# Products that nothing reads, put into TensorE's waits of a three-layer mixer network

## The chip, the cores and the metric

One core of one Trainium2 chip runs the whole network in one launch. The metric is the device time of an execution in microseconds; before the change it is 1105.38 us (median of 3 runs, 1104.76 to 1110.9).

## What is computed

One sequence of 256 tokens, width 1024, in f32, through three layers. Layer 0 ("first block") mixes with a gated linear recurrence, a gated linear attention and an eight-head block attention; layers 1 and 2 ("second block") mix with a delta-rule recurrence (RWKV-7), four heads of dilated attention and four heads of latent attention. Each layer ends in a gated feed-forward part of width 2816. Layer 0 norms what each half adds, layers 1 and 2 norm only what each half reads.

```python
def first_block(x, ...):                       # layer 0
    h = rms_norm(x, pre_mix_norm)
    x = x + rms_norm(hybrid_mixer(h, ...) @ w_out, post_mix_norm)
    h = rms_norm(x, pre_ffn_norm)
    f = (silu(h @ w_ffn_gate) * (h @ w_ffn_up)) @ w_ffn_down
    return x + rms_norm(f, post_ffn_norm)

def second_block(x, positions, ...):           # layers 1 and 2
    for l in range(2):
        h = rms_norm_2(x, attn_norm_g[l])
        pa, pb, pc = split_sizes(h @ w_in[l], (A_PROJ, B_PROJ, C_PROJ))
        y = [rwkv7_mixer(pa, ...), dilated_mixer(pb, ...), mla_mixer(pc, ...)]
        x = x + concatenate(y) @ w_out[l]
        h = rms_norm_2(x, ffn_norm_g[l])
        x = x + (silu(h @ ffn_w_gate[l]) * (h @ ffn_w_up[l])) @ ffn_w_down[l]
    return rms_norm_2(x, final_norm_g)
```

## The kernel before

Activations are held transposed, width on the 128 partitions in 8 tiles (`KT`), tokens (`T` = 256) in the free dimension. Each dense product with weights is made of three fp32r products (`product`, L433 to L442): high half of the weights by high half of the activations, high by low, low by high. The weights come from memory as 148 chunks of up to 1 MB (`STREAM`) through a ring of three buffers: SP issues the load, ACT writes the high half (`w_hi`, L1040), DVE the low half (`w_lo`, L1455; L2045 for the two halves of the first chunk), PE multiplies, and then the buffer is free again. The rest (inverse, heads, norm sums, rotations) is done in plain f32 products, each of which is two MATMUL records in the trace.

The order on each engine is written out by hand, one instruction list per engine, tied by step counters: `V` counts steps of DVE, `A` of ACT, `M` of PE. `pe.wait_ge(V.sem, V.at(...))` holds PE, and all behind it in PE's list, until DVE has marked that step.

- The start: `as_they_come` runs the first chunk's products as pairs of activation tiles and the halves of the chunk come in (L441).
- `norm_sum` (L462 to L471) sums squares over partitions with a product by ones; for "mixed" and "fed" in layer 0 it is followed by ACT's inverse root (L1052, L1054), DVE's norm, residual and low half (L1499, L1437, L1505), and then by the first products of the next part.
- `rwkv(l)` holds the recurrence. Eight 64x64 matrices per chunk of tokens are inverted by doubling, levels n = 1 to 5 in two groups q: first products (L817), then other work that `beside_inverse(l, n)` puts there, then the products L825 and L830, then DVE subtracts (L1437) and the next level may begin. At n = 2 the work beside is the latents' products `up(0)`, `up(1)` (L441), for which PE waits for `c_lo`; before them DVE splits a chunk and makes the latents' low half, after them it does rotations. Level 6 is L839 and L846.
- The heads: `attention(l, i)`, i = 0 to 9, is a pipeline over eight heads (`attend`): scores of head i (L989, L990 for the four narrow heads, L993 to L996 for the wide ones), three transposes of head i-1 (L564 to L566), values of head i-2 (L572, L573). Between scores and transposes DVE takes the maximum (L1560 to L1565), ACT the exponential (L1115, L1117), DVE scales (L1547 to L1551), and ACT copies the transposed rows (L1040). attention 0 to 3 stand beside levels 5 and 6 of the inverse, 4 to 6 around the first chunk of the state (c = 0; L876, L888/L889, L899/L901/L912/L913), 7 to 9 around the second.

Of the kernel before, what the change touches and what calls it, by code (L numbers as in the profile page):

```python
# [36 lines left out]
P = 128  # L37
D = 1024
KT = D // P
T = 256  # L40
# [184 lines left out]
def program(nc, ins, out, plan):  # L225


    with ExitStack() as ctx:
        def sb(name, shape, dt=F32):
            return ctx.enter_context(nc.sbuf_tensor(name, shape, dt))  # L230
# [90 lines left out]
        AT2 |= area(0, dict(att_l=(2, 384), att_p=(2, 384)))[0]  # L321
        cq_hi, cq_lo = h_hi[:, 0:3, :], h_lo[:, 0:3, :]
        small = sb("small", [P, 96])
        ANG, _ = area(8192 + T, dict(p=(T,), ang=(2, T), n=(T,)))
        pos = arena[:, 8192:8192 + T].bitcast(I32)

# [108 lines left out]
        def _(pe):  # L435
# [15 lines left out]
            H = [lambda k: h_hi[:, k, :], lambda k: h_lo[:, k, :]]  # L451
            MX = [lambda k: mix_hi[:, k, :], lambda k: mix_lo[:, k, :]]
            IDENT, ONES, BONES = C("ident"), C("ones"), C("bones")

            def norm_sum(l, what, into=6):

# [284 lines left out]
            def rwkv(l):  # L741
# [66 lines left out]
                    last.then_inc(M.sem, M.mark(l, "inv0", q))  # L808
                project(l, 8)
                for n in range(1, 6):  # L810
                    for q in range(2):

                        pe.wait_ge(V.sem, V.at(l, "inv_bt", n, q))
                        pe.wait_ge(A.sem, A.at(l, "inv0", q)) if n == 1 else pe.wait_ge(V.sem, V.at(l, "inv_x", n - 1, q))
                        for m in range(4 * q, 4 * q + 4):
                            for h in HALVES:
                                last = pe.matmul(quads(q)[h, m % 4, 0:64], BT[h, m, :], Xm[h, m, :],  # L817
                                                 start=True, stop=True)
                        last.then_inc(M.sem, M.mark(l, "inv_y", n, q))
                    beside_inverse(l, n)  # L820
                    for q in range(2):
                        pe.wait_ge(A.sem, A.at(l, "inv_y", n, q))
                        for m in range(4 * q, 4 * q + 4):
                            for h in HALVES:
                                last = pe.matmul(blocks(quads(2 + q)[h, m % 4, 0:64], n, 1), Y[h, m, :],  # L825
                                                 blocks(XT[h, m, :], n, 1), start=True, stop=True)
                        last.then_inc(M.sem, M.mark(l, "inv_zt", n, q))
                        for m in range(4 * q, 4 * q + 4):
                            for h in HALVES:
                                last = pe.matmul(blocks(quads(q)[h, m % 4, 0:64], n, 0), XT[h, m, :],  # L830
                                                 blocks(Y[h, m, :], n, 0), start=True, stop=True)
                        last.then_inc(M.sem, M.mark(l, "inv_z", n, q))
                    if n >= 5:
                        attention(l, 2 * n - 9)
# [32 lines left out]
                for c in range(TT):  # L867
# [11 lines left out]
                    if c:  # L879
                        mean_of(0)  # L880
                    attention(l, 4 + 3 * c)
                    pe.wait_ge(A.sem, A.at(l, "r", c))
                    if c == 0:
                        pe.wait_ge(V.sem, V.at(l, "inv_xt", 6, 1))
# [41 lines left out]
            def beside_inverse(l, n):  # L926

                b = AT2
                CQ = [lambda k: cq_hi[:, k, :], lambda k: cq_lo[:, k, :]]
                CKV = [lambda k: cq_hi[:, 2, :], lambda k: cq_lo[:, 2, :]]  # L930

                def up(i):


                    c = CHUNK[l, "uq" if i < 3 else "ukv", 0]
                    if i in (0, 3):
                        split(pe, c)
                    if i >= 2:
                        pe.wait_ge(A.sem, A.at(l, "up", i - 2))
                    if i < 3:  # L940
                        for t in range(2):
                            last = product(pairs(4 + i % 2)[:, t, :], tile_of(c, 2, 768, (2 * i + t) * P), range(2), CQ)
                    elif i < 5:
                        for t in range(2):
                            last = product(pairs(4 + i % 2)[:, t, :], tile_of(c, 1, 1024, (2 * (i - 3) + t) * P), [0],
                                           CKV)
                    else:
                        s, t = c % RING, i - 5
                        last = product(bank[4 + i % 2][:, :],
                                       [lambda k, p=p: p[:, 2, t * P:(t + 1) * P] for p in (cq_hi, cq_lo)], [0],  # L950
                                       [lambda k, p=p: p[:, s, 512:1024] for p in (w_hi, w_lo)])
                    last.then_inc(M.sem, M.mark(l, "up", i))

                if n == 1:

                    pe.wait_ge(V.sem, V.at(l, "in", 7))
                    pe.wait_ge(A.sem, A.at(l, "rkv"))
                    pe.wait_ge(A.sem, A.at(l, "kb_turned"))
                    pe.matmul(bank[6][:, :], C("rot_b"), B2["bq"].rearrange("p a b -> p (a b)"), start=True, stop=True)
                    pe.matmul(bank[7][:, :], C("rot_b"), B2["bk"].rearrange("p a b -> p (a b)"), start=True, stop=True)\  # L960
                        .then_inc(M.sem, M.mark(l, "b_rot"))
                if n == 2:
                    pe.wait_ge(V.sem, V.at(l, "c_lo"))
                    up(0)
                    up(1)
                if n == 3:

                    pe.wait_ge(V.sem, V.at(l, "rotated", 0))
                    pe.matmul(bank[6][:, 0:T], C("dup")[0:64, :], B2["krope"][0:64, :], start=True, stop=True)
                    pe.matmul(bank[6][:, T:2 * T], C("dup_rot")[0:64, :], B2["krope"][0:64, :], start=True, stop=True)\  # L970
                        .then_inc(M.sem, M.mark(l, "k_rot"))
                    for i in range(2, 5):
                        up(i)
                if n == 4:
                    pe.wait_ge(V.sem, V.at(l, "rotated", 1))
                    pe.matmul(bank[7][:, :], C("rot_c"), b["qr"].rearrange("p a b -> p (a b)"), start=True, stop=True)\
                        .then_inc(M.sem, M.mark(l, "q_rot"))
                    up(5)
                    up(6)
                if n >= 5:  # L980
                    attention(l, 2 * n - 10)

            def attention(l, i):
# [27 lines left out]
                    pe.wait_ge(V.sem, V.at(l, "b_lo"))  # L1011
                attend(l, i, 8, scores, value, out_bank)

            for l in range(LAYERS):
                if l:
                    pe.wait_ge(mats, 16 * l)
# [9 lines left out]
                        w_out(l, m, (0, 1) if m < 2 else range(KT))  # L1026
                if l == 0:
                    norm_sum(l, "mixed")
                ffn(l)
                if l == 0:  # L1030
                    norm_sum(l, "fed")
            norm_sum(LAYERS, "final")


# [396 lines left out]
        def _(dve):  # L1431
# [605 lines left out]
                    after_v("angles" if (i, s, n) == (1, 1, 7) else f"angle_{i}_{s}_{n}")  # L2037


            dve.wait_ge(x_loaded, 32)  # L2040
            def first_lo(h):

# [173 lines left out]
```

## Time and profile before

| what | value |
|---|---|
| median of 3 runs | 1105.38 us (1104.76 to 1110.9) |
| profiled execution, its own time | 1106.32 us |
| its span, first to last instruction | 1104.4 us |
| mean granted TensorE clock | 0.954 |
| PE, DVE, ACT busy | 95%, 62%, 46% |
| HBM read | 154 MB, 140 GB/s over the span |

The profile is of one execution. Its page has the busy times and, in 40 slices of 27.6 us, the granted clock (9 stands for 90% and more). A matmul's record is longer than the distance to the next one, since products are pipelined; the distance between starts is the pace. Lines are those of the kernel before.

### The profile page before, as it was taken

The numbers are of one execution on the slowest core, as the hardware profiler recorded it, in microseconds if no ns is written. First come the engines' busy times: TensorE is split into PE (matmuls) and PEld (weight loads), VectorE is DVE, ScalarE is ACT, GpSimd is POOL, SyncE is SP. The second block draws the span as 40 slices with busy tenths as digits, with TensorE's granted clock in tenths as the row PEclk, the third lists the DMA queues.
The fourth block names the chain that finished last, engine by engine and source line by source line (L and its number), as shares of the span: only waits on it lengthen the run. The fifth ranks groups of instructions, "written<-read, shape, count | busy, mean of one in ns | idle before, by whom it ended". The sixth has DMA issues, their size and how long they took to land. (4 is left out here: it accounts for less than half of the span.)

```text
span 1104.4 us, 20079 instructions
## 1 busy us (share of the span) xinstructions
PE 1052.7 (95%) x8728; PEld 989.1 (90%) x8728; DVE 684.1 (62%) x1079; ACT 503.8 (46%) x663; POOL 4.1 (0%) x9
## 2 busy tenths in 40 slices
PE   5999989999997998999999999999899999999996
PEld 5898889999997997769999999998776799999996
DVE  5867476775567877444665555579653456655554
ACT  5475464444436543233644443466233455444332
POOL 0000000000000000000000000000000000000000
PEclk9999999999999999579999999999985899999999
DMA  8444334555452322021455555533220135555531
GB/s 315 153 140 162 115 144 165 191 182 199 165 184 85 135 87 80 37 77 60 184 191 191 181 179 182 185 120 115 78 78 33 44 115 191 191 191 188 179 130 39
DMA packets 23736, 156.41 MB, mean 142 GB/s; under 512 B 2576, under 2 KB 3776, under 8 KB 6112
## 3 DMA queue, kind: packets, MB, share of 16 engines
q1 hardware_dynamic: 21600, 151.70, 38.2%
q10 hardware_dynamic: 1840, 2.50, 0.7%
q8 instruction: 69, 1.13, 0.4%
q0 software_dynamic: 208, 0.92, 0.3%
q14 instruction: 19, 0.16, 0.0%
HBM read 154.05 MB, written 1.06 MB: 140 GB/s over the span
## 5 line engine op out<-in xcount | busy, mean ns | idle before, releaser
L441 PE MATMUL bank<-h_hi,w_hi 128*128 128x256 f32 x1480 | 427.9, 289 | 26.8 <-DVE w_lo L2045 11.1
L1455 DVE TENSOR_TENSOR w_lo<-raw,w_hi 128x2048 fp32r<-128x2048 f32 (+3 forms) x144 | 323.5, 2251 | 179.6 <-ACT w_hi L1040 178.3
L441 PE MATMUL bank<-h_lo,w_hi 128*128 128x256 f32 x1480 | 422.4, 285 | 0.0
L441 PE MATMUL bank<-h_hi,w_lo 128*128 128x256 f32 x1480 | 422.1, 285 | 0.0
L441 PEld LDWEIGHTS bank<-h_hi,w_hi 128*128 128x128 f32 x1480 | 287.5, 194 | 32.3 <-issue 19.2
L1040 ACT ACTIVATE w_hi<-raw 128x2048 fp32r<-128x2048 f32 (+3 forms) x144 | 269.2, 1873 | 91.5 <-PE bank L441 86.4
L441 PEld LDWEIGHTS bank<-h_lo,w_hi 128*128 128x128 f32 x1480 | 287.7, 194 | 1.0 <-issue 0.7
L441 PEld LDWEIGHTS bank<-h_hi,w_lo 128*128 128x128 f32 x1480 | 287.6, 194 | 0.0
L441 PE MATMUL bank<-mix_hi,w_hi 128*128 128x256 f32 x720 | 205.3, 285 | 2.5 <-DVE mix_lo L1437 2.0
L441 PE MATMUL bank<-mix_lo,w_hi 128*128 128x256 f32 x720 | 203.7, 283 | 0.0
L441 PE MATMUL bank<-mix_hi,w_lo 128*128 128x256 f32 x720 | 203.7, 283 | 0.0
L441 PEld LDWEIGHTS bank<-mix_hi,w_hi 128*128 128x128 f32 x720 | 138.1, 192 | 4.8 <-DVE mix_lo L1437 3.1
L441 PEld LDWEIGHTS bank<-mix_lo,w_hi 128*128 128x128 f32 x720 | 138.1, 192 | 0.1
L441 PEld LDWEIGHTS bank<-mix_hi,w_lo 128*128 128x128 f32 x720 | 138.1, 192 | 0.0
L1138 ACT ACTIVATE arena<-arena 128x256 f32<-128x256 f32 x66 | 27.6, 418 | 195.6 <-DVE arena L1437 195.6
L1437 DVE TENSOR_TENSOR arena<-arena 128x256 f32<-128x256 f32 (+2 forms) x132 | 70.8, 543 | 44.1 <-ACT arena L1138 35.8
L1040 ACT ACTIVATE arena<-bank 128x256 f32<-128x256 f32 (+3 forms) x72 | 32.1, 448 | 127.1 <-PE bank L566 60.7
L1437 DVE TENSOR_TENSOR mix_lo<-arena,mix_hi 128x256 fp32r<-128x256 f32 (+1 forms) x70 | 30.7, 440 | 33.4 <-ACT mix_hi L1040 33.4
L1040 ACT ACTIVATE mix_hi<-arena 128x256 fp32r<-128x256 f32 (+1 forms) x70 | 30.1, 430 | 42.6 <-DVE arena L1437 36.9
L1437 DVE TENSOR_TENSOR arena<-bank,rstd 128x512 f32<-128x512 f32 x66 | 45.1, 684 | 0.0
L1075 ACT ACTIVATE h_hi<-x,par 128x256 fp32r<-128x256 f32 x44 | 19.6, 500 | 32.6 <-DVE x L1437 27.1
L1462 DVE SCALAR_TENSOR_TENSOR h_lo<-x,par,h_hi 128x256 fp32r<-128x256 f32 x44 | 20.3, 507 | 12.6 <-ACT h_hi L1075 12.6
(299 smaller groups left out, 935.8 us busy)
## 6 DMA issues: line engine op xcount, KB each, us to landing
raw<-in_w SPq DMA_DIRECT2D x136, 1024.0 KB, 4.8
raw<-in_w SPq DMA_DIRECT2D x5, 512.0 KB, 3.7
raw<-in_w SPq DMA_DIRECT2D x2, 896.0 KB, 4.5
raw<-in_w SPq DMA_DIRECT2D x2, 768.0 KB, 4.2
cst<-in_consts SPq DMA_DIRECT2D x1, 1314.0 KB, 12.7
x<-in_x SPq DMA_DIRECT2D x2, 512.0 KB, 6.0
arena<-bias_rows ACTq DMA_DIRECT2D x1, 1024.0 KB, 6.1
out<-arena ACTq DMA_DIRECT2D x4, 256.0 KB, 2.0
```

What stands on the lines that cost most here:

```text
L441: last = pe.matmul(dst, w[a](k), act[b](k), start=start and i == 0 and j == 0, stop=stop and i == n - 1 and j == 2, skip_group_check=loose)
L1040: return act.activation(dst, src, ACT.Copy, **kw)
L1075: last = act.activation(h_hi[:, k, :], x[:, k, :], ACT.Copy, scale=Par(g, k))
L1138: act.activation(FF["sg"][:, j % 2, :], FF["gu"][:, j % 2, 0, :], ACT.Silu)\
L1437: ins_ = dve.tensor_tensor(dst, a, b, op)
L1455: dve.tensor_tensor(w_lo[:, s, 0:n], raw[:, s, 0:n], w_hi[:, s, 0:n].bitcast(F32), ALU.subtract)\
L1462: last = dve.scalar_tensor_tensor(h_lo[:, k, :], x[:, k, :], Par(g, k), h_hi[:, k, :].bitcast(F32), ALU.mult, ALU.subtract)
```

## The change

A helper `keep_busy(n, operand, dst)` issues n plain f32 products of 128x128 by 128x256 into a PSUM bank whose contents nothing needs at that point; nothing reads the results. It is called at six places of PE's list:

- 13 products ahead of everything, on a tile that DVE clears first (`filler`, a part of the table of rotations that is written much later), behind a wait for that step;
- 6 each behind the two norm sums of layer 0;
- in layers 1 and 2: 5 at level 2 of the inverse ahead of the wait for `c_lo`, 5 ahead of the first products of level 5, 2 behind `attention(l, 4)` (in the first chunk of the state, c = 0).

All but the first 13 use the constants' tile as operand. DVE gets one memset as its first instruction. Nothing else is added, removed or moved.

```diff
+        filler = rope[:, 0, :]
...
+            def keep_busy(n, operand, dst):
+                for _ in range(n):
+                    pe.matmul(dst, operand[:, 0:P], operand[:, 0:T], start=True, stop=True)
...
                 project(l, 8)
                 for n in range(1, 6):
+                    if n == 5:
+                        keep_busy(5, cst, bank[6][:, 0:T])
                     for q in range(2):
                         pe.wait_ge(V.sem, V.at(l, "inv_bt", n, q))
...
                     attention(l, 4 + 3 * c)
+                    if c == 0:
+                        keep_busy(2, cst, bank[2][:, 0:T])
                     pe.wait_ge(A.sem, A.at(l, "r", c))
...
                 if n == 2:
+                    keep_busy(5, cst, bank[5][:, 0:T])
                     pe.wait_ge(V.sem, V.at(l, "c_lo"))
                     up(0)
...
+            pe.wait_ge(V.sem, V.at("filler"))
+            keep_busy(13, filler, bank[7][:, 0:T])
             for l in range(LAYERS):
...
                 if l == 0:
                     norm_sum(l, "mixed")
+                    keep_busy(6, cst, bank[7][:, 0:T])
                 ffn(l)
                 if l == 0:
                     norm_sum(l, "fed")
+                    keep_busy(6, cst, bank[7][:, 0:T])
...
+            dve.memset(filler, 0.0).then_inc(V.sem, V.mark("filler"))
             dve.wait_ge(x_loaded, 32)
```

## Rows read from the trace of the kernel before

**Rows 1.** The page: span, busy times, granted clock in slices, weight queue.

```profile
span 1104.4 us, 20079 instructions
...
PE 1052.7 (95%) x8728; PEld 989.1 (90%) x8728; DVE 684.1 (62%) x1079; ACT 503.8 (46%) x663; POOL 4.1 (0%) x9
...
PEclk9999999999999999579999999999985899999999
...
q1 hardware_dynamic: 21600, 151.70, 38.2%
```

**Rows 2.** Stretches: length, busy us (count) of PE, PEld, DVE, ACT, POOL, clock, DMA, GB/s.

```profile
180.00:190.00 10.00, 10.00 (x86) 10.00 (x85) 7.81 (x12) 5.48 (x5) 0.00 (x0) 1.00 0.66 251
...
422.86:426.27 3.41, 3.02 (x14) 3.02 (x15) 3.31 (x7) 0.06 (x1) 0.00 (x0) 0.50 0.86 293
446.75:484.30 37.55, 37.55 (x213) 27.14 (x213) 12.72 (x54) 13.52 (x36) 0.00 (x0) 0.50 0.08 29
...
818.81:859.77 40.96, 40.28 (x247) 29.75 (x247) 14.09 (x58) 14.03 (x37) 0.00 (x0) 0.50 0.08 27
...
sum 98.98, PE 97.37 PEld 75.42 DVE 40.45 ACT 34.21 POOL 0.00; mean PE 12.17 PEld 9.43 DVE 5.06 ACT 4.28 POOL 0.00
```

**Rows 3.** In order of time, at the start: start, length, work, [idle before].

```profile
11.13 0.55 PE L441 MATMUL bank<-h_hi,w_hi 128*128 128x256 f32 x1 [11.13 <-DVE w_lo L2045]
...
6.95 0.88 DVE L1462 SCALAR_TENSOR_TENSOR h_lo<-x,par,h_hi 128x256 fp32r<-128x256 f32 x2 [6.95 <-ACT h_hi L1075]
...
13.33 1.21 DVE L2045 TENSOR_TENSOR w_lo<-raw,w_hi 128x1024 fp32r<-128x1024 f32 x1
```

**Rows 4.** In order of time, PE in the inverse of layer 1.

```profile
415.85 1.12 PE L959 MATMUL bank<-arena,cst 128*128 128x512 f32 x2 [1.13 <-DVE arena L1531]
...
423.25 0.58 PE L441 MATMUL bank<-h_hi,w_hi 128*128 128x256 f32 x1 [2.01 <-DVE h_lo L1437]
...
445.28 1.31 PE L817 MATMUL bank<-arena 64*64 64x64 f32 x32 [2.02 <-DVEq L1937]
446.52 1.03 PE L989 MATMUL bank<-arena 64*128 64x256 f32 x2
```

**Rows 5.** In order of time, PE behind the norm sums of layer 0.

```profile
138.45 0.59 PE L468 MATMUL bank<-arena,cst 128*128 128x256 f32 x2
138.88 0.59 PE L470 MATMUL bank<-arena,cst 128*128 128x256 f32 x2
...
143.15 0.58 PE L441 MATMUL bank<-h_hi,w_hi 128*128 128x256 f32 x1 [3.24 <-DVE h_lo L1505]
147.63 0.39 PE L441 MATMUL bank<-h_hi,w_hi 128*128 128x256 f32 x1 [0.66 <-DVE h_lo L1462]
...
347.19 0.39 PE L441 MATMUL bank<-h_hi,w_hi 128*128 128x256 f32 x1 [2.05 <-DVE h_lo L1462]
```

**Rows 6.** In order of time, PE in the heads of layer 1.

```profile
453.04 0.47 PE L564 MATMUL bank<-cst,arena 128*128 128x128 f32 x1
...
473.17 0.47 PE L888 MATMUL bank<-arena 64*64 64x64 f32 x2
...
476.40 1.22 PE L993 MATMUL bank<-spare 128*128 128x256 f32 x2
...
480.15 0.47 PE L564 MATMUL bank<-cst,arena 128*128 128x128 f32 x1
...
488.50 0.33 PE L564 MATMUL bank<-cst,arena 128*128 128x128 f32 x1 [1.65 <-DVE arena L1551]
...
497.81 0.33 PE L564 MATMUL bank<-cst,arena 128*128 128x128 f32 x1 [0.64 <-DVE arena L1551]
```

**Rows 7.** In order of time, DVE: a subtraction of level 2, and one head's softmax.

```profile
428.86 0.48 DVE L1437 TENSOR_TENSOR arena<-arena,bank 128x128 f32<-128x128 f32 x2 [0.89 <-PE bank L830]
...
453.14 0.42 DVE L1560 CUSTOM_DVE_ANT_0 arena<-bank,cst 128x256 f32<-128x256 f32 x1 [0.18 <-PE bank L990]
...
455.84 0.28 DVE L1551 TENSOR_SCALAR arena<-arena,small 128x128 f32<-128x128 f32 x1
```

## The prediction

> **What bounds the kernel now.** I read the page first, for who is busy: TensorE (PE) is busy 95% of the span, VectorE (DVE) 62%, ScalarE (ACT) 46%, and the sixteen DMA engines 38% on the weight queue [rows 1]. So products set the time, and a change to PE's waits can only pay if it makes products faster or earlier. Next I read the row of the granted clock on the page, which drops in two places of the 40 slices, near 450 us and near 820 us [rows 1]. The table by stretch then gives the low spells exactly: eight of them, at half clock (1.2 GHz, against 2.4 elsewhere), 99.0 us together, and 78.5 of these lie in two spells of 37.6 and 41.0 us, one in each of the two recurrent layers, with PE busy through nearly all of them [rows 2]. A full stretch of dense products has 86 starts in 10 us, one every 0.117 us; in the low spell at 422.86 there are 14 in 3.02 us, one every 0.21 [rows 2]. So the low level costs a product of 256 columns some 0.095 us. A ninth spell is not in that table: from 11.13 us on [rows 3] the first 25 products start 0.21 us apart, up to 16.6 us, and 0.12 after it, so PE begins at 1.2 GHz as well.
>
> What PE did before each fall is the third view, its instructions in order of time. Ahead of 446.75 stands a wait of 2.02 us (445.28, for DVE's last subtraction of the level before), ahead of 422.86 one of 2.01 us (for the low half of the latents) [rows 4]; the spells at 818.81 and 798.33 in layer 2 have the same two waits ahead, within 0.02 us. Ahead of 142.97 stands one of 3.24 us and ahead of 347.77 one of 2.05 us [rows 5]. A wait of 1.13 us at 415.85 was followed by no fall, but one of 0.64 us at 497.81, behind small products, was [rows 4, 6]. So a wait of 2 us costs the clock nearly each time, one of about 1 us sometimes. The long spells are another matter: after one 2-us wait the clock stays low for 37 us although PE records no wait [rows 2], so the light products of the inverse and the heads (64 rows or 64 columns) do not bring it back at 1.2 GHz; only the denser products of the first chunk's output, which end at 484.7 us, do.
>
> **Price of an added product.** It is a plain f32 product of 128x256, the same form as the four of the norm sum, two of which start 0.43 us apart at 2.4 GHz [rows 5], so 0.86 us at 1.2 GHz. Five take 2.15 us, six 2.6, two 0.86 (1.7 if low).
>
> **Part 1, 13 ahead of the first product.** PE idles until 11.13 us, when the first half of w_lo is there [rows 3]. The fillers need only a memset on a DVE that is idle until 6.95 us [rows 3], so I let them start near 1.2 us (an estimate from the first ACT and SP records of 0.75 us). All at 1.2 GHz they take 11.2 us and end at 12.4, 1.2 us late. If the clock rises after some 5.5 us of them, as it did after 5.5 us of real products, 6.4 of them go at 0.86 and 6.6 at 0.43: end near 9.5 us, in time, with 1.6 us of waiting left, a wait of the size that sometimes costs the clock. Gain if it holds: 25 products x 0.095 = 2.4 us, of which 0.6 is lost again, since the 25th product now waits for the second half of w_lo (13.33 + 1.21 = 14.54 us, against 11.13 + 24 x 0.117 = 13.94) [rows 3]. So 1.8 saved at best, 1.2 lost at worst; I take 1.5 saved. DVE and ACT run ahead of PE here, since PE waits for neither again before 90 us.
>
> **Part 2, six behind each norm sum of the first layer.** They run 2.6 us inside idle time of 3.24 us (3.29 behind the second sum) that ends with DVE's chain of norm, residual and low half [rows 5]: no cost. But the gain is small too. At 143 us the low spell costs nothing, because PE then waits 0.66 us for the next low half anyway (147.63). At 347 us the fall follows the second wait of 2.05 us, behind which no filler stands [rows 5]. With the first spell warm, that second wait appears at 145 us as well. I take 0, and -1 to +1.5 us for the range.
>
> **Part 3, five ahead of the latents' products, level 2, in two layers.** Filler 2.15 us in a wait of 2.01: 0.14 us late. It should keep 2.4 GHz for the 14 products that now run low [rows 2], 16 in layer 2: 1.3 and 1.5 us. Yet DVE is busy with rotations until 0.89 us before it begins the level's subtraction at 428.86 [rows 7]; more than that cannot be passed on. Net 0.8 us a layer, 1.6 together.
>
> **Part 4, five ahead of level 5, and two in the heads.** The wait of 2.02 us is covered, again 0.14 us late, so the fall at 446.75 and 818.81 goes. How long does the clock then hold? I laid the work behind it out at 2.4 GHz. PE's pieces: level-5 first products 1.24 us (445.28 to 446.52, still warm) [rows 4]; 64 small products 1.9, which is what they take at level 1 (417.76 to 419.65); a narrow head's scores 0.8, half of 1.58 low; three transposes 0.38; values 0.75; a wide head's scores 1.9, half of 3.75 low (476.40 to 480.15); the state's eight pairs 2.0, an estimate between half and the whole of 3.23 low (473.17 to 476.40) [rows 6]. Against it stands the softmax on DVE and ACT, 3.0 us from its first logits to its last scaled row (453.14 to 456.12) [rows 7], which is now hidden because PE is slow. So new waits appear. The transposes of head 0 can start at 447.35 + 3.0 + 0.5 (two subtractions ahead in DVE's queue) = 450.85, where PE is free at 450.05; they now start at 453.04: 2.2 us earlier [rows 6]. Head 1: one turn of DVE, ACT, DVE later, 453.9 against 457.34: 3.4 us. Head 2: 457.85 against 463.11, 5.3 us. Head 3: 461.8 against 470.87, 9.1 us. Head 5, behind two splits of weights (1.90 us on ACT and 2.29 on DVE each) in their queues: 477.8 against 488.50, 10.7 us, or 9.8 after the two fillers [rows 6]. (The starts of heads 1 to 3 are from the same view; rows 6 has head 0, 4, 5 and 6.) The waits ahead of heads 0, 1 and 2 come out at 0.8 to 1.1 us, the size at which both outcomes were seen, and they lie among light products. What is gained is kept when the clock falls, since PE is then again alone on the path. So per layer: 2.2 if it falls at head 0, 3.4 at head 1, 5.3 at head 2, 9.8 if never. I take 4.4, between heads 1 and 2. The two products in the heads cost 1.7 us when low; if they lift the clock, they return 1.2 (eight pairs) + 1.8 (wide scores) + 0.45 (transposes) = 3.4 us; with even odds that is 0.
>
> A rule bears on this. The transposes of the heads are a third of the pieces there, and no row tells their weight for the clock apart from their neighbours'. The Trainium skill, page "TensorE: Matmul & The Clock Gate", section "Part 4: PE-mode transpose", says that transposes do not count as PE being busy in the way other products do. By that rule the clock falls early among the heads, which is the second rival below, 1101.3 us against the forecast's 1093.5.
>
> **Sum.** 1.5 + 0 + 1.6 + 2 x 4.4 = 11.9 us off the profiled span of 1104.4, which is 1092.5; the profiled execution took 1106.32, 1.9 more than its span and 0.9 more than the median of 1105.38. Against that median I forecast 1093.5 us. Nothing behind it should eat the gain: in a feed-forward part PE is full while DVE is busy 7.8 us of 10 and the DMA engines 66% [rows 2], so earlier products find their weights.
>
> **Rivals.**
> - *The clock holds through the heads* (both layers, warm to head 5). For it: from 484.3 to 497.9 heads run at 2.4 GHz with a wait of 1.65 us among them, ahead of 488.50 [rows 6]. 1.5 + 1.6 + 2 x 9.8 = 22.7 us: 1082.7 us. Chance 0.15.
> - *It falls at head 0 and the two products in the heads do not lift it.* 1.5 + 1.6 + 2 x 2.2 - 2 x 1.7 = 4.1 us: 1101.3 us. For it: the 0.64-us wait that was enough at 497.81 [rows 6]. Chance 0.17. The skill's rule on transposes, above, points the same way.
> - *Slower: products that nothing reads do not hold the clock.* Then each is only queue time. At the start 13 x 0.86 end at 12.4 us, +1.2; at the inverse 4 x 0.14 = +0.6; in the heads 2 x 1.7 = +3.4: 1110.6 us. It decides from the point where the first product starts after 11.13 us. Against it: real f32 products of the same form stand in warm stretches, and nothing in a product's record tells whether its result is read. The trace has no product on zeros, and the ones at the start are on zeros. On zeros the Trainium skill says, same page, section "Seeing it yourself", that they do not trip the peak-current limiter; that is another throttle, but it shows that operands can matter. Chance 0.05.
> - The forecast itself (falls somewhere at heads 1 to 3): 1088 to 1099 us. Chance 0.61. The 0.02 left is for a path I have not seen.
>
> **Range and chances.** From the warm rival's 1082.7, widened by the uncertain first two parts to 1081, up to the second rival's 1101.3, to 1102 us. About 0.5% (5.5 us, the point at 1099.9) is what a measurement of this kernel can tell from no change. Faster: 0.61 + 0.15 and a fifth of the second rival, 0.80. Same: 0.15. Slower: 0.05.
>
> **What would show it.** Right: no low spell at 423, 798, 447 and 819 us; first products 119 ns apart at 11.13 us; low time of the spells in the recurrent layers down from 78.5 to some 50 us; waits of about 1 us before the heads' transposes. Wrong in the first part: first product after 11.2 us, or 213 ns apart. Wrong in the third: the wait at the level's subtraction on DVE unchanged. Wrong in the fourth: low from 447 us again (the filler does not hold it), or a single low slice left (it holds throughout). The prediction falls if the two long spells begin where they do now.

## The result, and the profile after

The changed kernel takes 1100.00 us, median of 11 runs (1097.76 to 1101.97), against 1107.41 for the kernel before (1104.76 to 1111.08, 11 runs): a ratio of 0.9927 with a 95% interval of 0.9910 to 0.9943. It is 7.4 us faster; the sum had 11.9. The two profiled executions are 1106.32 and 1101.32 us, with spans of 1104.4 and 1099.5, so the traces show 4.9 us of the gain; the mean granted clock goes from 0.954 to 0.963.

The page of the changed kernel, answering to [rows 1]:

```profile
span 1099.5 us, 20276 instructions
...
PE 1067.3 (97%) x8826; PEld 998.5 (91%) x8826; DVE 684.3 (62%) x1080; ACT 503.8 (46%) x663; POOL 4.3 (0%) x9
...
PEclk9999999999999999669999999999995999999998
```

PE shows 98 more matmul records and 14.6 us more busy time in a span 4.9 us shorter. The two dips of the clock are still there; the second now shows in one slice instead of three.

The low spells of the changed kernel, in the view and with the columns of [rows 2]:

```profile
345.30:348.71 3.41, 3.41 (x16) 3.41 (x17) 3.05 (x7) 2.01 (x4) 0.00 (x0) 0.50 0.00 0
447.69:481.83 34.14, 33.82 (x147) 23.31 (x147) 11.03 (x44) 12.28 (x31) 0.00 (x0) 0.50 0.09 31
485.24:488.65 3.41, 3.17 (x14) 2.98 (x14) 1.35 (x7) 1.84 (x6) 0.00 (x0) 0.50 0.66 274
823.16:853.88 30.72, 30.48 (x127) 20.39 (x127) 10.38 (x36) 10.91 (x27) 0.00 (x0) 0.50 0.10 35
857.29:860.71 3.42, 3.42 (x17) 3.25 (x16) 1.03 (x4) 1.84 (x6) 0.00 (x0) 0.50 0.51 213
1089.40:1092.81 3.41, 3.41 (x8) 2.17 (x7) 0.00 (x0) 0.00 (x0) 0.00 (x0) 0.50 0.00 0
...
sum 78.51, PE 77.71 PEld 55.52 DVE 26.85 ACT 28.89 POOL 0.00; mean PE 12.95 PEld 9.25 DVE 4.47 ACT 4.82 POOL 0.00
```

Low time fell from 98.98 to 78.51 us. The spells at 143, 423 and 798 us are gone; the last two were forecast to go. The two long ones shrank from 37.6 and 41.0 us to 34.1 and 30.7, together 64.9 where some 50 was forecast, and a spell has come at the end, at 1089 us.

To find where the time went I looked up the start of the same product in both traces, place by place. PE of the changed kernel, in order of time (columns as in [rows 3]; a row "bank<-cst" with no idle before it is the added products, two records for each):

```profile
1.19 8.92 PE L460 MATMUL bank<-rope 128*128 128x256 f32 x26 [1.19 <-DVE rope L2056]
11.01 0.35 PE L442 MATMUL bank<-h_hi,w_hi 128*128 128x256 f32 x1 [0.90 <-DVE w_lo L2062]
14.52 0.35 PE L442 MATMUL bank<-h_hi,w_hi 128*128 128x256 f32 x1 [0.41 <-DVE w_lo L2062]
...
145.71 0.39 PE L442 MATMUL bank<-h_hi,w_hi 128*128 128x256 f32 x1 [2.08 <-DVE h_lo L1478]
345.25 0.57 PE L442 MATMUL bank<-h_hi,w_hi 128*128 128x256 f32 x1 [2.06 <-DVE h_lo L1478]
...
419.24 2.43 PE L460 MATMUL bank<-cst 128*128 128x256 f32 x10
421.32 0.46 PE L442 MATMUL bank<-h_hi,w_hi 128*128 128x256 f32 x1
440.19 2.43 PE L460 MATMUL bank<-cst 128*128 128x256 f32 x10
448.01 0.48 PE L571 MATMUL bank<-cst,arena 128*128 128x128 f32 x1 [0.63 <-DVE arena L1567]
468.15 2.08 PE L460 MATMUL bank<-cst 128*128 128x256 f32 x4
470.15 0.47 PE L899 MATMUL bank<-arena 64*64 64x64 f32 x2
...
820.90 0.33 PE L571 MATMUL bank<-cst,arena 128*128 128x128 f32 x1 [0.64 <-DVE arena L1567]
823.68 0.47 PE L571 MATMUL bank<-cst,arena 128*128 128x128 f32 x1 [0.24 <-DVE arena L1567]
839.51 2.08 PE L460 MATMUL bank<-cst 128*128 128x256 f32 x4
841.52 0.47 PE L899 MATMUL bank<-arena 64*64 64x64 f32 x2
1089.20 1.07 PE L474 MATMUL bank<-arena,cst 128*128 128x256 f32 x2 [2.10 <-DVE arena L1453]
```

The same places in layer 2 and at the end of the kernel before, which [rows 6] does not hold:

```profile
819.49 0.80 PE L817 MATMUL bank<-arena 64*64 64x64 f32 x10 [2.00 <-DVEq L1937]
...
828.09 0.47 PE L564 MATMUL bank<-cst,arena 128*128 128x128 f32 x1
...
832.39 0.47 PE L564 MATMUL bank<-cst,arena 128*128 128x128 f32 x1
...
848.23 0.47 PE L888 MATMUL bank<-arena 64*64 64x64 f32 x2
...
1095.73 0.70 PE L467 MATMUL bank<-arena,cst 128*128 128x256 f32 x2 [2.11 <-DVE arena L1437]
```

| place | before | after | ahead by |
|---|---|---|---|
| 25th product | 16.39 | 14.52 | 1.9 |
| second feed-forward norm, next product | 347.19 | 345.25 | 1.9 |
| latents' first product, layer 1 | 423.25 | 421.32 | 1.9 |
| last step of level 4, layer 1 | 441.20 | 438.21 | 3.0 |
| level 5, layer 1 | 445.28 | 442.55 | 2.7 |
| head 0, transposes | 453.04 | 448.01 | 5.0 |
| state's pairs, behind the heads' two products | 473.17 | 470.15 | 3.0 |
| a wide head's transposes | 488.50 | 485.48 | 3.0 |
| first products of level 2, layer 2 | 793.68 | 790.62 | 3.1 |
| last step of level 4, layer 2 | 815.43 | 811.09 | 4.3 |
| level 5, layer 2 | 819.49 | 815.43 | 4.1 |
| head 0, layer 2 | 828.09 | 820.90 | 7.2 |
| head 1, layer 2 | 832.39 | 823.68 | 8.7 |
| state's pairs, layer 2 | 848.23 | 841.52 | 6.7 |
| final norm sum | 1095.73 | 1089.20 | 6.5 |
| end of the span | 1104.4 | 1099.5 | 4.9 |

Read down the last column, the table says where each part paid: 1.9 at the start; nothing behind the norm sums; 1.1 and 1.3 from level 2; 0.3 given back in each layer ahead of level 5, where the five products end later than the wait did; 2.3 and 4.65 behind the start of level 5; then 2.0 given back in each layer between head 1 and the state's pairs, where the heads' two products stand; and 1.6 given back at the very end.

### The profile page after: what moved, and what is told of

Same layout as the page of the kernel before. It is cut to its first block and busy times, and to the rows that moved or that the text cites. A ratio compares the mean times of both kernels' runs of the same rounds, so it can differ in the third digit from the quotient of the medians.

```text
span 1099.5 us, 20276 instructions
## 1 busy us (share of the span) xinstructions
PE 1067.3 (97%) x8826; PEld 998.5 (91%) x8826; DVE 684.3 (62%) x1080; ACT 503.8 (46%) x663; POOL 4.3 (0%) x9
## 5 line engine op out<-in xcount | busy, mean ns | idle before, releaser
L442 PEld LDWEIGHTS bank<-h_hi,w_hi 128*128 128x128 f32 x1480 | 284.4, 192 | 15.1 <-issue 7.4
L442 PEld LDWEIGHTS bank<-h_lo,w_hi 128*128 128x128 f32 x1480 | 284.4, 192 | 1.0 <-issue 0.7
L442 PEld LDWEIGHTS bank<-h_hi,w_lo 128*128 128x128 f32 x1480 | 284.4, 192 | 0.0
L1453 DVE TENSOR_TENSOR mix_lo<-arena,mix_hi 128x256 fp32r<-128x256 f32 (+1 forms) x70 | 30.7, 440 | 33.3 <-ACT mix_hi L1056 33.3
L1091 ACT ACTIVATE h_hi<-x,par 128x256 fp32r<-128x256 f32 x44 | 19.5, 500 | 32.5 <-DVE x L1453 27.1
```

What stands on the lines that cost most here:

```text
L442: last = pe.matmul(dst, w[a](k), act[b](k), start=start and i == 0 and j == 0, stop=stop and i == n - 1 and j == 2, skip_group_check=loose)
L1091: last = act.activation(h_hi[:, k, :], x[:, k, :], ACT.Copy, scale=Par(g, k))
L1453: ins_ = dve.tensor_tensor(dst, a, b, op)
```

## The experiments

Two theories ran against each other at first. T: the gain is the clock held past level 5, it ends at the first small wait among the light products of the heads, and the heads' two products cost more than they return. H: the heads' two products lift the clock and belong to the gain. All ratios are to the kernel before on the same chip. In the table "gain" is (1 - ratio) x 1107 us, with the same done to the interval; it can differ from the difference of two medians by about 1 us.

| run | median us (n) | ratio, 95% | gain, us |
|---|---|---|---|
| the change | 1100.00 (11) | 0.9927, 0.9910 to 0.9943 | 8.1, 6.3 to 10.0 |
| e1_no_heads | 1098.26 (6) | 0.9915, 0.9896 to 0.9933 | 9.4, 7.4 to 11.5 |
| e2_only_n5 | 1100.66 (6) | 0.9932, 0.9917 to 0.9947 | 7.5, 5.9 to 9.2 |
| e3_only_start | 1106.74 (12) | 0.9996, 0.9982 to 1.0010 | 0.4, -1.1 to 2.0 |
| e4_only_heads | 1107.70 (12) | 1.0002, 0.9988 to 1.0016 | -0.2, -1.8 to 1.3 |
| e5_only_n2 | 1103.22 (12) | 0.9960, 0.9947 to 0.9974 | 4.4, 2.9 to 5.9 |
| e7_hold | 1081.44 (5) | 0.9756, 0.9730 to 0.9782 | 27.0, 24.1 to 29.9 |
| e8_hold_more | 1079.38 (4) | 0.9744, 0.9719 to 0.9769 | 28.3, 25.6 to 31.1 |
| e11_n5_hold | 1084.48 (6) | 0.9788, 0.9759 to 0.9817 | 23.5, 20.3 to 26.7 |
| e12_hold_only | 1093.60 (6) | 0.9895, 0.9857 to 0.9934 | 11.6, 7.3 to 15.8 |
| e13_hold_one | 1080.74 (5) | 0.9764, 0.9738 to 0.9790 | 26.1, 23.2 to 29.0 |

All of them compute everything that the reference asks for; they differ only in the added products.

**The heads' two products taken out of the change.**

```diff
                     attention(l, 4 + 3 * c)
-                    if c == 0:
-                        keep_busy(2, cst, bank[2][:, 0:T])
```

> The changed kernel without the two products in the heads (c = 0); all other added products stay. Theory T: these two only take queue time, 2.0 us in each of layers 1 and 2 at the low level, and do not lift the clock, so this kernel is about 4 us faster than the changed one: 11 us under the kernel before, ratio near 0.990. Rival H: in most executions they lift the clock in the heads and the profiled execution was an unlucky one; then this kernel is slower than the changed one, ratio to the kernel before 0.995 or more.

1098.26 us, 1.7 below the change by the medians, with intervals that overlap. So the two products bring nothing that can be seen here, and may cost a little. T had 4 us, H a ratio of 0.995 or more, which lies outside the interval (0.9896 to 0.9933): that speaks against H.

**Level 5 alone.** The kernel before with only this:

```diff
                 for n in range(1, 6):
+                    if n == 5:
+                        keep_busy(5, cst, bank[6][:, 0:T])
```

> The kernel before with only the five products ahead of level 5 of the inverse, in both layers. Theory T: the fall moves from the wait ahead of level 5 to the first waits of the heads, 2 to 4 us saved a layer, 4 to 7 in all, ratio near 0.995. Rival: the clock falls among the light products anyway at the same place, nothing saved, ratio 0.999 to 1.001.

1100.66 us, a gain of 7.5: as much as the whole change, and a little more than T had. In its trace the clock held past a wait of 0.64 us ahead of head 0, and the long spell of layer 1 begins at 453.98, in a wait of 0.32 us ahead of head 1, and not at 446.75.

**The start alone.** The kernel before with the memset and the 13 products ahead of the first layer:

```diff
+            pe.wait_ge(V.sem, V.at("filler"))
+            keep_busy(13, filler, bank[7][:, 0:T])
             for l in range(LAYERS):
```

> The kernel before with only the 13 products on zeros ahead of the first product. Theory T: the first products run at 2.4 GHz and the 1.9 us saved by the 25th product stays to the end, ratio near 0.998. Rival: DVE or the loads give it back later, or the 1.6 us of waiting left costs the clock in other executions, ratio 0.9995 to 1.001.

1106.74 us; a gain of 0.4 that can't be told from none. PE at its start, in order of time:

```profile
1.19 7.34 PE L460 MATMUL bank<-rope 128*128 128x256 f32 x26 [1.19 <-DVE rope L2049]
...
11.41 0.55 PE L442 MATMUL bank<-h_hi,w_hi 128*128 128x256 f32 x1 [2.88 <-DVE w_lo L2055]
```

In this execution the 13 products ended at 8.53 and left a wait of 2.88 us, and the real products start at the low pace again (0.21 us from the second to the third). In the profile of the change the same 26 records took 8.92 us, the wait was 0.90, and the products were fast. So this part works in some executions and is too short in others.

The other traces show how often. Seven traces have the 13 products at the start: in three of them the first 24 real products all ran at the high pace (the change, e1_no_heads, e7_hold), in two the clock fell after 11 or 12 (e10_after_again, e8_hold_more), and in two it was low from the first (this one and e13_hold_one). In the seven without them the first 13 to 27 products are at the low pace. The 25th product starts at 14.52 to 15.91 us with them, 15.33 in the mean, and at 15.25 to 16.39 without, 15.83 in the mean. So the part is worth some 0.5 us, and the 1.9 us of the table above comes from setting the best of the seven beside the worst.

**The heads' two products alone**, on the kernel before.

```diff
                     attention(l, 4 + 3 * c)
+                    if c == 0:
+                        keep_busy(2, cst, bank[2][:, 0:T])
```

> The kernel before with only the two products in the heads, in both layers. Theory T: 2.0 us a layer lost, clock low through the heads as before, 4 us slower, ratio near 1.0035. Rival H: the clock rises behind them in one or both layers and 1 to 6 us are saved, ratio 0.995 to 0.999.

1107.70 us, no change. Neither theory had it right, and the trace shows how that can be (it is of the slowest of the 12 executions, 1111.49 us). The stretches around them in layer 1, columns as in [rows 2], and PE at the wait behind:

```profile
444.64:475.37 30.73, 30.37 (x188) 22.64 (x188) 9.27 (x46) 10.71 (x31) 0.00 (x0) 0.50 0.00 1
475.37:485.61 10.24, 9.13 (x73) 6.07 (x71) 6.13 (x11) 3.62 (x8) 0.00 (x0) 1.00 0.28 102
485.61:506.08 20.47, 18.22 (x65) 13.66 (x67) 6.38 (x27) 4.38 (x14) 0.00 (x0) 0.50 0.14 53
```

```profile
473.74 1.92 PE L459 MATMUL bank<-cst 128*128 128x256 f32 x4
...
487.75 0.48 PE L570 MATMUL bank<-cst,arena 128*128 128x128 f32 x1 [3.25 <-DVE arena L1559]
```

Here the two products did lift the clock, 1.6 us after they began and nine us before it rises without them ([rows 2], 484.30). It then stayed high only to the wait of 3.25 us ahead of the wide head's transposes, which are even later than the 1.65 us of [rows 6] because PE arrived there sooner, and a new low spell of 20.5 us followed. In layer 2 it went the same way, on a smaller scale: products at 852.08, the clock up at 854.24, a wait of 3.25 us, low again from 864.48 to 871.31. Lifted, and given back.

**Level 2 alone**, on the kernel before.

```diff
                 if n == 2:
+                    keep_busy(5, cst, bank[5][:, 0:T])
                     pe.wait_ge(V.sem, V.at(l, "c_lo"))
```

> The kernel before with only the five products ahead of the latents' products (level 2), in both layers. Theory T: 0.8 to 1.2 us a layer passed on, 2 us in all, ratio 0.998. Rival: the spell moves to the wait ahead of level 5 or is given back there, as the spells in the first chunk did in the run with the products in the heads alone: ratio 0.9995 to 1.001.

1103.22 us, a gain of 4.4, more than T gave it, and more than the 1.1 and 1.3 us that level 2 pays in the profile of the change. Its trace has no spells at 421 and 796 us, and also none of the short ones near 498 and 863; the long one of layer 1 has the old length (445.09 to 482.63), that of layer 2 is 37.6 us instead of 41.0 (817.14 to 854.69). That these others are missing too need not be the work of level 2: the spell near 863 is missing in e3_only_start as well, and its long spells differ from [rows 2] in length.

**Holding the clock in the heads.** If the layout at 2.4 GHz was right, it should be possible to have what the first rival promised, by covering the small waits ahead of the transposes of heads 0 to 2 with two products each, and leaving out the two in the heads:

```diff
                     j = i - 1
+                    if l and j < 3:
+                        keep_busy(2, cst, bank[7][:, 0:T])
                     pe.wait_ge(V.sem, V.at(l, "probs", j))
```

> The changed kernel without the two products in the heads, and with two added products ahead of the wait for the scaled rows of heads 0, 1 and 2 in layers 1 and 2 (the waits of 0.6 to 1.1 us that appear when the clock is high). Theory T: the small waits among light products are what makes the clock fall behind level 5, so covering them holds it for heads 0 to 3 at least: 3 to 6 us a layer beyond the kernel without them, ratio 0.979 to 0.986. Rival: the products of inverse and heads are too light to hold the clock even without waits, or the six products cost what they bring (0.86 us a pair if they don't fit): ratio 0.990 to 0.993, as without them.

1081.44 us: 26 us under the kernel before, more than T had. Stretches of this kernel in layer 1 (in layer 2 one spell is left, 832.45 to 835.86):

```profile
446.75:477.46 30.71, 25.82 (x222) 19.15 (x219) 16.64 (x64) 13.68 (x37) 0.00 (x0) 1.00 0.15 49
477.46:480.87 3.41, 3.41 (x16) 3.32 (x15) 0.71 (x2) 1.89 (x7) 0.00 (x0) 0.50 0.43 183
487.70:491.11 3.41, 3.41 (x17) 2.68 (x17) 0.00 (x0) 0.49 (x1) 0.00 (x0) 0.50 0.02 5
```

PE in its heads of layer 1:

```profile
448.94 1.13 PE L460 MATMUL bank<-cst 128*128 128x256 f32 x4
449.91 0.27 PE L573 MATMUL bank<-cst,arena 128*128 128x128 f32 x1
...
452.25 1.13 PE L460 MATMUL bank<-cst 128*128 128x256 f32 x4
...
468.66 0.33 PE L573 MATMUL bank<-cst,arena 128*128 128x128 f32 x1 [1.66 <-DVE arena L1567]
476.66 0.33 PE L573 MATMUL bank<-cst,arena 128*128 128x128 f32 x1 [3.22 <-DVE arena L1567]
```

The clock is high from level 5 to 477.46, through the three transposes of each head and even past a wait of 1.66 us. PE is now idle for 4.9 us of those 30.7, and these are the two waits shown, ahead of the transposes of the first two wide heads: there DVE and ACT bound it. In heads 0 to 2 two products take 0.97 us from the first to the transposes, and no wait is left ahead of these.

**More of it**, in the same place with two of the wide heads and the final norm added (the edit is shown against e7_hold):

```diff
                     j = i - 1
-                    if l and j < 3:
-                        keep_busy(2, cst, bank[7][:, 0:T])
+                    fill = {0: (2, 7), 1: (2, 7), 2: (2, 7), 5: (3, 0), 7: (1, 0)}.get(j) if l else None
+                    if fill:
+                        keep_busy(fill[0], cst, bank[fill[1]][:, 0:T])
...
+            keep_busy(4, cst, bank[7][:, 0:T])
             norm_sum(LAYERS, "final")
```

> As e7_hold, and also three products ahead of the scaled rows of head 5, one ahead of those of head 7 and four ahead of the final norm sum, where PE waits 2.1 us. Theory T: another 1 to 3 us, since the short spells near 485 and 857 us and the one at the final norm sum go: ratio 0.976 to 0.983. Rival: these waits cost the clock only in part of the executions and the added products lengthen the path by 0.5 to 1 us: no difference from e7_hold.

1079.38 us, the fastest kernel of the study, all runs within 1079.36 and 1080.04; 2.1 us under the last one, with intervals that overlap. From 446 to 500 us the clock is at 1.00 throughout; in layer 2 it is low from 828.72 to 835.54, from a wait of 1.67 us of the kind that it held past in layer 1.

**One product for each head instead of two** (against e7_hold).

```diff
                     if l and j < 3:
-                        keep_busy(2, cst, bank[7][:, 0:T])
+                        keep_busy(1, cst, bank[7][:, 0:T])
```

> The holding kernel with one product in place of two ahead of the scaled rows of heads 0, 1 and 2. Theory T: half of a wait of 0.9 to 1.1 us stays open, and as a wait of 0.6 us behind light products was already followed by a fall, the clock falls at one of them in part of the executions: ratio 0.977 to 0.985, with a wider scatter than with two. Rival: the first part of the wait is what counts and one product is enough: ratio 0.974 to 0.977, as with two.

1080.74 us, the same as with two. T expected a wider scatter and missed. PE in heads 0 and 1 of layer 1:

```profile
449.69 0.70 PE L460 MATMUL bank<-cst 128*128 128x256 f32 x2
450.40 0.33 PE L573 MATMUL bank<-cst,arena 128*128 128x128 f32 x1
...
452.79 0.70 PE L460 MATMUL bank<-cst 128*128 128x256 f32 x2
453.33 0.27 PE L573 MATMUL bank<-cst,arena 128*128 128x128 f32 x1
```

The transposes start 0.71 and 0.54 us behind the one product, 0.54 again at head 2, and no wait is recorded ahead of them. So no half of a wait was left open, as T thought: these waits are no longer than about 0.7 us, not 0.8 to 1.1. The second product of e7_hold is only queue time. Head 3's transposes start 16.27 us behind the start of level 5 here, and 17.33 in e7_hold.

**Level 5 and the heads' waits, nothing else**, on the kernel before.

```diff
+                    if n == 5:
+                        keep_busy(5, cst, bank[6][:, 0:T])
...
+                    if l and j < 3:
+                        keep_busy(2, cst, bank[7][:, 0:T])
```

> The kernel before with only the five products ahead of level 5 and the two each ahead of the scaled rows of heads 0, 1 and 2, in layers 1 and 2. Theory T: these two together carry nearly all of the gain of the holding kernel (2.4%), the start, the norm sums and level 2 bring 1 to 3 us more: ratio 0.977 to 0.981. Rival: the waits are one chain and each gap left open, that at level 2 above all, costs the clock for the whole inverse: ratio 0.985 or more.

1084.48 us: 22 of the 26 us, as T had it. The other parts together are worth some 3 us on top by the medians, though the intervals overlap (20.3 to 26.7 and 24.1 to 29.9).

**The heads' waits without level 5**, on the kernel before (the second pair of lines above alone).

> The kernel before with only the two products each ahead of the scaled rows of heads 0, 1 and 2. Theory T: the clock is low before them, since the wait of 2 us ahead of level 5 is open; at the low level there are no waits for them to fill, so they take 6 x 2 x 0.86 to 1.0, 10 to 12 us, unless they lift the clock; with a lift in half of the cases 0 to 5 us remain: ratio 0.997 to 1.010. Rival: they lift the clock nearly always, and the heads run high from head 1 on: ratio 0.985 or less.

1093.60 us, between what the two theories gave, and the runs spread from 1091.32 to 1103.48. The profile is of one of the two long ones, 1101.34 us; the other four stand at 1091 to 1094. Stretches of it:

```profile
444.82:472.13 27.31, 27.10 (x176) 21.23 (x177) 8.22 (x41) 7.33 (x24) 0.00 (x0) 0.50 0.00 1
...
823.71:833.95 10.24, 10.24 (x91) 8.53 (x88) 3.31 (x17) 2.13 (x7) 0.00 (x0) 0.50 0.01 2
```

The clock fell at level 5, in the wait of 2.00 us that ends at 445.03. In layer 1 the pairs of added products, at 453.63, 459.75 and 467.33, all ran low, and the clock came back at 472.13, behind the third and twelve us earlier than in [rows 2]; in layer 2 it was low for only 10.2 us. So these products can lift the clock as well as hold it, if less surely and late. At 1.2 GHz they stood in no wait, so if they lifted it, it was by the work that they added and not by a gap closed.

**The same two kernels looked at again.** One more execution of each.

> The kernel before, unchanged, profiled a second time. Theory T: where the clock falls differs from one execution to the next by up to 3 us, so the short spells (near 143, 348, 423, 498, 798, 863 us) are not all in the same place or number, while the two long ones begin ahead of or at level 5 in both. Rival: the spells stand at the same places within 0.3 us, and differences between kernels can be read spell by spell.

> The changed kernel, unchanged, profiled a second time. Theory T: the place at which the clock falls behind level 5 differs from the first profile by up to 3 us, and whether the two products in the heads lift it too; the long spells are 27 to 37 us again. Rival: the same places within 0.3 us.

The kernel before, 1104.25 us, with the stretches that differ from [rows 2]:

```profile
140.88:147.71 6.83, 5.37 (x23) 5.08 (x24) 6.51 (x15) 2.74 (x6) 0.00 (x0) 0.50 0.00 0
...
444.67:482.21 37.54, 37.54 (x212) 27.14 (x213) 12.69 (x53) 13.53 (x36) 0.00 (x0) 0.50 0.08 29
```

The changed kernel, 1099.22 us, both long spells, and the heads' products in layer 1:

```profile
450.11:470.59 20.48, 20.48 (x81) 14.29 (x81) 5.55 (x29) 8.47 (x25) 0.00 (x0) 0.50 0.00 1
...
822.17:852.89 30.72, 30.72 (x128) 20.57 (x127) 10.16 (x37) 10.95 (x28) 0.00 (x0) 0.50 0.10 35
```

```profile
469.45 1.68 PE L460 MATMUL bank<-cst 128*128 128x256 f32 x4
```

Where the clock falls and rises is not a fixed property of the kernel. Part of the difference in time is the whole trace shifted: level 5 of the kernel before starts at 443.21 us in this execution and at 445.28 in the first. Set against the work, six of its eight spells stand where they stood, and two do not: the one at the first norm sum begins 1.0 us sooner in the wait and lasts twice as long, and the next begins at 342.27, behind the wait of 3.29 us, not behind the one of 2.05. In layer 1 of the changed kernel head 0's transposes start 1.7 us later than in the first profile (449.67); the clock fell 0.44 us behind them and not 0.32 ahead of them, and the heads' two products, at 469.45, lifted it; in layer 2 they did not. T had long spells of 27 to 37 us, and one is 20.5. Still the long spell of the kernel before begins with level 5 in both executions.

The gains of the parts do not add: start, level 2, level 5 and heads alone give 0.4 + 4.4 + 7.5 - 0.2 = 12.1, and together 8.1. The difference of 4.0 is hardly more than the intervals of the five gains leave open (some 3.6 together, an estimate), and what makes it is not shown.

## Why the prediction was right and where it was off

**That unread products hold the clock: right.** The first real product at 11.01 us is followed by others 0.12 us apart, where they were 0.21 apart [rows 3], though what stood ahead of it were products on zeros. The low spells at 423 and 798 us are gone, and in e7_hold the clock stays high for the 30.7 us that were low before. The slower rival, at 1110.6 us, falls.

**Part 1: 1.5 forecast, 1.9 in the profile, but some 0.5 over the traces and 0.4 (-1.1 to 2.0) in e3_only_start.** That the profile agrees is luck. The term was worked out as one case, with the wait left behind it (1.6 us) noted as one that sometimes costs the clock. It was 0.90 in one trace and 2.88 in another, and in the second the clock had fallen. The other side of the sum was a single case too: 25 products at the low pace, where other executions have as few as 13. The step that was missing is to weigh the term by these chances. The 25th product waited for the second half of w_lo as forecast (14.52 against 14.54).

**Part 2: 0, right**, and for the reason given: with the spell at 143 gone, the second wait came out at 145.71, 2.08 us long, and took back what the high clock had won. The lead is 1.9 us there as ahead of it. The spell at the second norm sum stayed (345.30), in the second wait.

**Part 3: 1.1 and 1.3, forecast 0.8 each.** The latents' first product began exactly as far ahead as the work before it (1.93), so the 0.14 us of lateness was not there. In layer 1 PE met DVE where [rows 7] said it would: DVE goes from its rotations into the level's subtraction with no idle time.

```profile
425.36 0.69 DVE L1453 TENSOR_TENSOR arena<-spare 128x512 f32<-128x512 f32 x1
426.09 0.48 DVE L1453 TENSOR_TENSOR arena<-arena,bank 128x128 f32<-128x128 f32 x2
```

**Part 4: the step that was off.** It had 4.4 us a layer, 8.8 together, and the trace shows 2.3 - 2.0 and 4.65 - 2.0, that is 2.9, less the 0.3 a layer by which the five products end late (0.14 forecast): 2.4.
- The fall at level 5 went, as forecast. The gain at each place is near what the layout gave: 2.3 us where it falls at head 0 (2.2 forecast), 4.65 where it falls at head 1 (3.4 forecast; 0.8 of the difference is that in the kernel before the clock of layer 2 fell ahead of level 5's products, and that of layer 1, for which the layout was made, behind them). But the place was taken one head too late: between heads 1 and 2, because waits of 0.8 to 1.1 us were laid out there. The waits that came ahead of head 0 were 0.63 and 0.64 us. In layer 1 the clock fell in the first of these (447.69, head 0 starts at 448.01); in layer 2 it fell at 823.16, 2.3 us behind the second, ahead of head 1. The row that showed it was in hand: the 0.64-us wait at 497.81 [rows 6]. Even so it is no rule: in e2_only_n5 the clock came through head 0's wait of 0.64 us and fell at head 1, and in the changed kernel it held past the 0.64-us wait that ends at 496.31.
- The heads' two products were put at 0, as even odds between -1.7 and +1.7. They lifted the clock in neither layer of this profile and cost 2.0 each, since the next start is 2.00 us behind them, so 1.0 for a product at 1.2 GHz and not 0.86. Taken over all traces the odds and the return were about right: of the six layers with these products (the change and e10_after_again, e4_only_heads) the clock rose in three. There PE won, from head 3 to head 5 and with the products' own time taken off, 1.3 and 1.1 us in e4_only_heads against the kernel before, and 1.6 in e10_after_again against the first profile (1.7 forecast). What the sum left out is what comes behind head 5: in layer 1 of e4_only_heads the clock fell there for 20.5 us, and by head 7 PE was 5.6 us behind the kernel before.

Of the two, only the first is clear of the scatter; e1_no_heads and e4_only_heads put the second at 1.3 and 0.2 us lost, either within its interval.

**The final norm sum: not foreseen.** It now runs low behind a wait of 2.10 us, where it ran at full speed behind 2.11. ScalarE had its sum 6.53 - 4.89 = 1.6 us later than the lead of PE would give. The prediction said that nothing behind the sum eats the gain; a wait of 2 us on the path should have been on that list. It is no effect of the change: six of the 14 traces have a spell there (the others are e1_no_heads, e2_only_n5, e3_only_start, e5_only_n2 and e11_n5_hold), and eight have none, e10_after_again, e7_hold and e13_hold_one among them. What decides it is open. So the four products that e8_hold_more has ahead of it are not shown to be needed.

```profile
1092.87 0.47 ACT L1068 ACTIVATE rstd<-bank,cst 128x256 f32<-128x256 f32 x1 [4.38 <-PE bank L478]
```

**The whole.** 1100.00 us is inside the range, just outside the 1088 to 1099 us of the main case, and 1.3 us from the second rival. The gain is 7.4 us for 11.9. Term by term the profile has 1.9 + 0 + 2.3 + 2.4 and 1.6 lost at the end, 5.0, where the sum had 1.5 + 0 + 1.6 + 8.8: most of what is missing is part 4. The kernel before has a median of 1107.41 us over 11 runs, 2.0 above the one that the forecast was taken from.

**The rivals.** The changed kernel lies between the forecast and the second rival (1101.3): it did fall at head 0 in one layer, and the heads' products did not lift it. For the first rival, that the clock holds through the heads, the condition failed and the working held. With its waits covered, e7_hold came to 1081.44 us where it had 1082.7, and the wide head's transposes moved from 488.50 to 476.66, 11.8 us. Of these, 1.1 were there ahead of level 5 (its products began at 444.19 against 445.28), which leaves 10.7, the number of the layout. To the tenth that is luck: the layout had no added products in the heads, and in e13_hold_one, with one in place of two, these transposes start 31.6 us behind the start of level 5, against 32.5 in e7_hold and in the layout.

**The rule on transposes.** In e7_hold the clock stayed at 1.00 through heads 0 to 2, with three transposes each and the added products ahead of them, and also at heads 3 and 4 (461.52 and 468.66), which have none added. So the transposes alone did not bring it down in this trace. By the Trainium skill ("TensorE: Matmul & The Clock Gate", section "Part 4: PE-mode transpose") they don't count as PE being busy as other products do; the runs neither show nor contradict that. That the clock fell at head 0 is no proof of the rule.

**What no run separates.** An added product does two things at once in the heads: it closes a small wait, and it puts a dense product among light ones. The holding kernels change both, and in e4_only_heads, where no wait stood at that place, the second alone went with a rise of the clock in both layers, 1.6 and 2.2 us behind the start of the products. Which of the two keeps it high in e7_hold is not shown.

## What to carry to other kernels

Where TensorE's clock falls, look at all the waits of the light stretch behind the large one: covering only the large wait moves the fall to one of the next small ones (7.4 us gained here), covering the small ones too keeps the clock for most of the stretch (26 us), and in this kernel one unread product in each was as good as two. Put such products ahead of waits that are there when the clock is high, lay the stretch out at the high clock to find them, and don't put them where PE is already alone on the path, for there each is 1 us of queue. Look at more than one execution before you give a price to a single spell.

## What the runs showed of the hardware

- Among small products, the clock fell in a wait of 0.63 us (head 0, 447.69), 2.3 us behind one of 0.64 us (823.16) and in one of 0.32 us (453.98 in e2_only_n5), though it held past one of 1.66 us in layer 1 of e7_hold; in layer 2 of e8_hold_more it fell in such a one, of 1.67 us (828.72). The length of the wait alone does not tell.
- The mix of the inverse and the heads, much of it products of 64 rows or columns, keeps PE's record full at 1.2 GHz without bringing the clock back: 34.1 us with PE busy 33.8. Two dense products can bring it back: it rose 1.6 and 2.2 us after their start in the two layers of e4_only_heads, 1.1 us in layer 1 of e10_after_again; not in the three other cases.
- Products on zeros raise the clock (13 at the start, then a pace of 0.12 us in five of seven traces, 0.21 in the other two, where a wait of 2.87 or 2.88 us came between).
- An added product of 128x256 in f32 has two records. Ten of these took 2.43 us at 2.4 GHz, 0.49 a product; four took 2.08 at 1.2 GHz, 1.0 a product.
- The same kernel has its low spells at partly other places of its work in another execution: behind the wait of 2.05 us at the second norm sum (347.77) or behind the one of 3.29 us before it (342.27, e9_before_again); ahead of head 0's transposes (447.69) or behind them (450.11, e10_after_again).
